# The state-space scan of a hybrid decoder layer: which operand of its last product stands still in TensorE

## The chip, the cores and the metric

The kernel runs on 1 core of one Trainium2 chip. The metric is the device time of one execution in microseconds (us). Every time and row below is of the kernel before the change.

## What is computed

One layer of 256 tokens and 1024 channels: a half-weighted SwiGLU block, a mixer, a second half-weighted SwiGLU block and a final norm. The mixer projects the normalised input once and feeds 8 attention heads and 16 state-space heads of 64 channels; their outputs are gated, normalised and projected back. The change lies in the state-space heads:

```
a     = dt * A                      # per token and head; dt the step, A negative
decay = exp(segsum(a))              # decay[l, s] = exp(cs[l] - cs[s]) for s <= l, 0 above
CB    = einsum('bclgn,bcsgn->bgcls', C, B)
y     = einsum('bgrcls,bcsgrp->bclgrp', CB * decay, x * dt)
y     = y + x * D_skip
y     = y * silu(z)                 # then normalised by group of 8 heads
```

Here cs is the running sum of a over the tokens. With one chunk of 256 tokens the carried states add nothing. All of it is float32.

## The kernel before, in words

Every engine runs one written-out list of work, and semaphores join the lists. The order within a list is the order of execution. The time is mostly weight products on TensorE. Each weight is split into a high and a low part in a type of reduced precision (fp32r), and each product is three matmuls (helper `three`, L1606 to L1608). ACT writes the high part (L634), VectorE the low part (L1085).

The mixer's weights come in 44 half chunks, m = 0 to 43, 1024 columns each. All engines step through m. In the part of interest, m = 20 to 31, one half chunk is 12 matmuls of 512 columns on TensorE (`chunk_half`), and the splits run four steps ahead. Between the half chunks the rest of the mixer is put in: the scan, the transposes of q and k behind m = 22 and 26, the transposes of the gated output behind 27, the attention scores from 28 on.

The scan works on two heads behind each half chunk, m = 20 to 27. For head h there are three 128 by 128 tiles of a triangular matrix: tokens s on partitions, tokens l along columns, the first tile row with both l tiles (256 columns), the second with one (128 columns), 384 columns in all.

- ACT, `decay_exp`: two Relus (L935) make the arguments, one exponential (L939) the decay. Buffers `decay[:, h % 2, :]`. The row cs (`cs_row`) was stored and read back by POOL's queue, spread over all partitions. In step m this stands behind the high split.
- VectorE, `weigh`: two operations (L1472) multiply C B, the step of token s, and the decay, into `mix_m[:, h % 2, :]`. In step m this stands behind the low split, but ahead of it in m = 24.
- TensorE, `ssd_out`: three f32 matmuls a head (L1892 to L1894). A tile of `mix_m`, 128 columns, stands still and 64 columns of `x_tok` move. The outputs, tokens on partitions, fill banks 6 and 7, eight heads a block.
- VectorE, `ssd_add`: in m = 24 and 28 it adds a block of eight heads to x times D_skip (L1481), which POOL wrote (L603). `ssd_gate` (L1489) multiplies by silu(z), and `mix_scale` (L1497) is the norm's last step; the transposes behind m = 27 wait for it.

POOL's queue holds, in this order: the mask of C B, the store and the spreading of cs, four products with D_skip, the rotation of q, the rotation of k.

An f32 matmul leaves two LDWEIGHTS and two MATMUL records in the trace, here called parts; an fp32r matmul and an f32 transpose leave one of each.

Of the kernel before, what the change touches and what calls it, by code (L numbers as in the profile page):

```python
# [17 lines left out]
P = 128  # L18
# [77 lines left out]
def build(nc, x_in, w1s, w3s, w2s, norms, w_in, conv_w, conv_b, dt_bias, A_log, D_skip,  # L96
# [4 lines left out]
    with ExitStack() as ctx:  # L101
# [56 lines left out]
        with ExitStack() as mixer:  # L158
            xbc, qT, kT = (mixer.enter_context(nc.sbuf_tensor(name, shape, f32)) for name, shape in (
                ("xbc", [P, CT, SEQ]), ("qT", [P, HEADS // 2, SEQ]), ("kT", [P, HEADS // 2, SEQ])))  # L160
        sums_hi = sb("sums_hi", [P, 3, 512], f32r)
# [16 lines left out]
        G_BANK, U_BANK = 4, 5  # L178
        PAIR_T_BANK = 6
# [103 lines left out]
        x_tok_ready = sem("x_tok_ready")  # L283
        skip_ready = sem("skip_ready")
        proj_out = sem("proj_out")
        decay_arg = sem("decay_arg")
        decay_ready = sem("decay_ready")
        m_ready = sem("m_ready")
        y_done = sem("y_done")
        y_added = sem("y_added")  # L290
# [169 lines left out]
        def _(pool):  # L460
# [139 lines left out]
            for t in range(TT):  # L600
                for j in range(2):
                    pool.wait_ge(x_tok_ready, 2 * j + t + 1)
                    pool.tensor_tensor(  # L603
                        normed[:, t, D_ATTN + j * 512:D_ATTN + (j + 1) * 512].rearrange("p (h d) -> p h d", d=SP_),
                        x_tok[:, t, j * 512:(j + 1) * 512].rearrange("p (h d) -> p h d", d=SP_),
                        skip16[:, 8 * j:8 * j + 8].unsqueeze(2).to_broadcast([P, 8, SP_]), ALU.mult).then_inc(skip_ready, 1)
            pool.wait_ge(consts_loaded, 16)
            pool.wait_ge(proj_out, 4)
            rotate(q_tok)
            pool.wait_ge(proj_out, 6)  # L610
# [18 lines left out]
        def _(act):  # L629
# [297 lines left out]
            def decay_exp(h0):  # L927

                if h0 % 4 == 0:
                    act.wait_ge(cs_loaded[h0 // 4], 16)  # L930
                for h in (h0, h0 + 1):
                    if h >= 2:
                        act.wait_ge(m_ready, 2 * (h - 1))
                    for s, (a, b) in enumerate(((0, 256), (256, 384))):
                        act.activation(decay[:, h % 2, a:b], cs_row(h)[:, s * P:], ACT.Relu,  # L935
                                       bias=dts[:, 7, s, h:h + 1], scale=-1.0).then_inc(decay_arg, 1)
                for h in (h0, h0 + 1):
                    act.wait_ge(decay_arg, 2 * (h + 1))
                    act.activation(decay[:, h % 2, :], decay[:, h % 2, :], ACT.Exp, scale=-1.0).then_inc(decay_ready, 1)  # L939
# [35 lines left out]
            for m in range(5, MIX_HALVES):  # L975
# [11 lines left out]
                if m in (29, 31, 32):  # L987
                    h = {29: 0, 31: 4, 32: 6}[m]
                    softmax_exp(h)
                    softmax_exp(h + 1)  # L990
                for split in splits(m):
                    mix_hi(split)
# [20 lines left out]
                if 20 <= m < 28:  # L1013
                    decay_exp(2 * (m - 20))
                if m == 20:
                    for t in range(TT):
                        chunk_out("q", t, ACT.Copy, q_tok)
# [52 lines left out]
        def _(dve):  # L1070
# [368 lines left out]
            def cumsum_T_out():  # L1439
                dve.wait_ge(csT_done, 1)  # L1440
                dve.tensor_copy(csT[:, :], bank[0:SH, 7, 0:SEQ]).then_inc(csT_ready, 1)
# [20 lines left out]

            def weigh(h):

                g = h // 8
                if h == 0:
                    dve.wait_ge(cb_masked, 2)
                if h >= 2:
                    dve.wait_ge(y_done, h - 1)
                dve.wait_ge(decay_ready, h + 1)  # L1470
                for s, (a, b) in enumerate(((0, 256), (256, 384))):
                    dve.scalar_tensor_tensor(mix_m[:, h % 2, a:b], cb[:, g, a:b], dts[:, 6, s, h:h + 1],  # L1472
                                             decay[:, h % 2, a:b], ALU.mult, ALU.mult).then_inc(m_ready, 1)

            def ssd_add(g):

                cols = slice(D_ATTN + 512 * g, D_ATTN + 512 * (g + 1))
                dve.wait_ge(y_done, 8 * (g + 1))
                dve.wait_ge(skip_ready, 4)
                for t in range(TT):  # L1480
                    dve.tensor_tensor(normed[:, t, cols], bank[:, 6 + t, :], normed[:, t, cols], ALU.add).then_inc(y_added, 1)  # L1481

            def ssd_gate(g):

                cols = slice(D_ATTN + 512 * g, D_ATTN + 512 * (g + 1))
                for t in range(TT):
                    dve.wait_ge(y_added, 2 * g + t + 1)
                    dve.wait_ge(proj_out, 8 if g else 2)
                    dve.tensor_tensor(normed[:, t, cols], normed[:, t, cols], z_silu[:, t, 512 * g:512 * (g + 1)],  # L1489
                                      ALU.mult).then_inc(gated, 1)  # L1490
# [36 lines left out]
            for m in range(5, MIX_HALVES):  # L1527
                if m in (24, 28):
                    ssd_add(m // 4 - 6)
# [3 lines left out]
                if m == 24:  # L1533
                    weigh(8)
                    weigh(9)
# [15 lines left out]
                if 20 <= m < 28 and m != 24:  # L1551
                    weigh(2 * (m - 20))
                    weigh(2 * (m - 20) + 1)
# [49 lines left out]
        def _(pe):  # L1603
# [281 lines left out]
            def ssd_out(h):  # L1885
                pe.wait_ge(m_ready, 2 * (h + 1))
                if h == 0:
                    pe.wait_ge(x_tok_ready, 4)
                if h == 8:
                    pe.wait_ge(y_added, 2)  # L1890
                m, c, o = mix_m[:, h % 2, :], slice(h * SP_, (h + 1) * SP_), slice((h % 8) * SP_, (h % 8 + 1) * SP_)
                pe.matmul(bank[:, 6, o], m[:, 0:P], x_tok[:, 0, c], start=True, stop=True)  # L1892
                pe.matmul(bank[:, 7, o], m[:, P:SEQ], x_tok[:, 0, c], start=True, stop=False)  # L1893
                pe.matmul(bank[:, 7, o], m[:, SEQ:SEQ + P], x_tok[:, 1, c], start=False, stop=True).then_inc(y_done, 1)  # L1894
# [42 lines left out]
            def pv(h):  # L1937
                pe.wait_ge(probsT_ready, h + 1)
                if h == 0:
                    pe.wait_ge(proj_out, 10)  # L1940
                    pe.wait_ge(y_added, 4)
                pt, c = probsT[:, h, :], slice(h * HD, (h + 1) * HD)
                pe.matmul(bank[:, 6, c], pt[:, 0:P], v_tok[:, 0, c], start=True, stop=True)
                pe.matmul(bank[:, 7, c], pt[:, P:SEQ], v_tok[:, 0, c], start=True, stop=False)
                pe.matmul(bank[:, 7, c], pt[:, SEQ:SEQ + P], v_tok[:, 1, c], start=False, stop=True).then_inc(pv_done, 1)
# [42 lines left out]
            for m in range(M_CONV, M_OUT + 8):  # L1988
# [16 lines left out]
                if m == 18:  # L2005
                    x_transposes(1)
                if 20 <= m < 28:
                    ssd_out(2 * (m - 20))
                    ssd_out(2 * (m - 20) + 1)
# [121 lines left out]
```

## Time and profile before

| what | us |
|---|---|
| median of 3 runs | 550.88 (550.64 to 551.34) |
| profiled execution | 551.28 |
| its span, from first to last instruction | 549.5 |
| TensorE busy | 535.8 |
| VectorE busy | 434.7 |
| ACT busy | 339.4 |

The trace is of one execution. TensorE's matmuls overlap, so the distance from one start to the next says more than a duration. In a row, `128*128 128x512` are the rows and columns that stand still and the shape of what moves; `x4` merges four records, and then the time is from the first start to the last end. PEld is TensorE loading what stands still.

### The profile page before, as it was taken

How to read it: one execution, taken by the hardware profiler on the slowest of the kernel's cores; microseconds unless marked ns; L12 is line 12 of the kernel's file. 1: busy time of each engine (PE TensorE's matmuls, PEld its weight loads, DVE VectorE, ACT ScalarE, POOL GpSimd, SP SyncE). 2: the span in 40 equal slices, each digit the busy share in tenths (PEclk: the TensorE clock that was granted, in tenths of full speed). 3: DMA queues.
4: the chain of work that ended last, by engine and by line, in shares of the span. 5: the costliest groups of instructions: out<-in, count | busy, mean ns of one | idle time of the engine just before them, and what ended most of it. 6: DMA issues, size and time to landing. Idle time of an engine off the chain costs nothing.

```text
span 549.5 us, 9708 instructions
## 1 busy us (share of the span) xinstructions
PE 535.8 (98%) x3637; PEld 491.1 (89%) x3637; DVE 434.7 (79%) x657; ACT 339.4 (62%) x553; POOL 68.6 (12%) x104
## 2 busy tenths in 40 slices
PE   8999999999999989999999999999999999999994
PEld 6999899999999968998888788889999999999993
DVE  4899888889888695778768756599998988888855
ACT  7856466556655565766988864477566556556533
POOL 2003000000000330343741102000000000000015
PEclk9999999999999999999999999999999999999998
DMA  9866955557765327458626244265675557755202
GB/s 269 293 229 217 306 188 196 173 174 227 229 178 183 98 80 228 154 177 287 227 79 229 78 151 155 79 207 166 211 256 188 174 177 229 229 177 182 98 1 76
DMA packets 69966, 99.70 MB, mean 181 GB/s; under 512 B 1941, under 2 KB 55393, under 8 KB 69938
## 3 DMA queue, kind: packets, MB, share of 16 engines
q1 hardware_dynamic: 68336, 94.48, 52.7%
q0 software_dynamic: 1456, 4.59, 2.7%
q8 instruction: 16, 0.26, 0.2%
q10 hardware_dynamic: 146, 0.27, 0.1%
q14 instruction: 12, 0.10, 0.0%
HBM read 98.27 MB, written 1.06 MB: 181 GB/s over the span
## 4 chain that ended last, share of the span: by engine, by line
PE 84%; DVE 6%; DMA 3%; ACT 2%; POOL 2%; issue 2%; SPq 0%; POOLq 0%; DVEq 0%; ACTq 0%
PE bank L1606 26%; PE bank L1607 25%; PE bank L1608 25%; DMA raw<-in_ffn_w 3%; PE bank L1747 1%; DVE w_lo L1085 1%; DVE x L1102 1%; PE bank L1893 1%; PE bank L1894 1%; POOL x L549 1%; PE bank L1892 1%; POOL rstd L482 1%; ACT w_hi L634 1%; PE bank L1933 0%; DVE hT_lo L1148 0%
## 5 line engine op out<-in xcount | busy, mean ns | idle before, releaser
L1606 PE MATMUL bank<-hT_hi,w_hi 128*128 128x256 f32 x736 | 208.7, 284 | 0.8 <-DVE tok_rows L1253 0.7
L1607 PE MATMUL bank<-hT_lo,w_hi 128*128 128x256 f32 x736 | 208.1, 283 | 0.0
L1608 PE MATMUL bank<-hT_hi,w_lo 128*128 128x256 f32 x736 | 208.1, 283 | 0.0
L1085 DVE TENSOR_TENSOR w_lo<-raw,w_hi 128x1024 fp32r<-128x1024 f32 x128 | 158.2, 1239 | 23.4 <-ACT w_hi L634 22.7
L634 ACT ACTIVATE w_hi<-raw 128x1024 fp32r<-128x1024 f32 x128 | 134.0, 1055 | 40.4 <-PE bank L1608 25.6
L1606 PEld LDWEIGHTS bank<-hT_hi,w_hi 128*128 128x128 f32 x736 | 140.9, 191 | 3.5 <-DVE tok_rows L1253 1.7
L1607 PEld LDWEIGHTS bank<-hT_lo,w_hi 128*128 128x128 f32 x736 | 141.0, 192 | 1.5
L1608 PEld LDWEIGHTS bank<-hT_hi,w_lo 128*128 128x128 f32 x736 | 141.0, 192 | 0.0
L1606 PE MATMUL bank<-w_hi,hT_hi 128*128 128x512 f32 (+1 forms) x192 | 70.5, 367 | 1.8 <-DVE hT_lo L1148 0.7
L1608 PE MATMUL bank<-w_hi,hT_lo 128*128 128x512 f32 (+1 forms) x192 | 68.2, 355 | 0.0
L1607 PE MATMUL bank<-w_lo,hT_hi 128*128 128x512 f32 (+1 forms) x192 | 68.0, 354 | 0.0
L751 ACT ACTIVATE conv_acc<-bank 128x256 f32<-128x256 f32 x40 | 15.4, 384 | 63.1 <-PE bank L1608 63.1
L549 POOL TENSOR_TENSOR x<-x_tok,x 128x512 f32<-128x512 f32 x7 | 11.4, 1645 | 303.8 <-ACT x_tok L746 297.3
L1201 DVE TENSOR_TENSOR sums_lo<-x_tok,sums_hi 128x1536 fp32r<-128x1536 f32 x20 | 35.1, 1757 | 12.1 <-ACT sums_hi L716 11.9
L1606 PEld LDWEIGHTS bank<-w_hi,hT_hi 128*128 128x128 f32 x192 | 36.3, 189 | 8.1 <-issue 2.5
L1608 PEld LDWEIGHTS bank<-w_hi,hT_lo 128*128 128x128 f32 x192 | 36.3, 189 | 5.2
L716 ACT ACTIVATE sums_hi<-x_tok 128x1536 fp32r<-128x1536 f32 x20 | 29.7, 1486 | 17.4 <-PE bank L1608 17.4
L1607 PEld LDWEIGHTS bank<-w_lo,hT_hi 128*128 128x128 f32 x192 | 36.4, 190 | 4.3
L1253 DVE TENSOR_TENSOR tok_rows<-bank,conv_acc 128x256 f32<-128x256 f32 x40 | 16.8, 421 | 18.4 <-ACT conv_acc L751 18.4
L1606 PE MATMUL bank<-w_hi,gu_hi 128*128 128x512 f32 x76 | 29.8, 393 | 0.0
L1607 PE MATMUL bank<-w_lo,gu_hi 128*128 128x512 f32 x76 | 29.8, 392 | 0.0
L1608 PE MATMUL bank<-w_hi,gu_lo 128*128 128x512 f32 x76 | 29.6, 389 | 0.0
(223 smaller groups left out, 804.9 us busy)
## 6 DMA issues: line engine op xcount, KB each, us to landing
raw<-in_ffn_w SPq DMA_DIRECT2D x54, 1024.0 KB, 5.4
raw<-in_w_in SPq DMA_DIRECT2D x16, 1024.0 KB, 5.5
tok_rows<-in_ffn_w SPq DMA_DIRECT2D x10, 1024.0 KB, 5.3
raw<-in_w_out SPq DMA_DIRECT2D x6, 1024.0 KB, 4.9
raw<-in_ffn_w SPq DMA_DIRECT2D x8, 256.0 KB, 5.3
x<-in_x SPq DMA_DIRECT2D x4, 256.0 KB, 4.0
norm_w<-cs_heads POOLq DMA_DIRECT2D x2, 512.0 KB, 5.0
out_x<-normed SPq DMA_DIRECT2D x3, 256.0 KB, 2.3
```

What stands on the lines that cost most here:

```text
L482: pool.tensor_tensor(rstd[:, r:r + 1], row_mean[:, r:r + 1], minus_half[:, :], ALU.pow).then_inc(rstd_ready, 1)
L549: pool.tensor_tensor(xs, w2_sum[:, part, :], xs, ALU.add).then_inc(folded, 1)
L634: act.activation(by_tile(dst) if columns else dst, src, ACT.Copy).then_inc(hi_ready, 1)
L716: act.activation(sums_hi[:, :, :], w2_sum[:, 0:3, :], ACT.Copy).then_inc(sums_hi_ready, 1)
L751: act.activation(silu_g, bank[:, GU_BANK, 0:SEQ], ACT.Silu).then_inc(silu_ready, 1)
L1085: dve.tensor_tensor(lo, src, hi, ALU.subtract).then_inc(half_ready, 1)
L1102: dve.scalar_tensor_tensor(xs, bank[:, 2 * t + c, :], 1.0 if n == 2 else 0.5, xs, ALU.mult, ALU.add).then_inc(x_ready, 1)
L1201: dve.tensor_tensor(sums_lo[:, :, :], w2_sum[:, 0:3, :], sums_hi[:, :, :].bitcast(f32), ALU.subtract).then_inc(sums_ready, 1)
L1253: dve.tensor_tensor(gu[:, odd, :], bank[:, GU_BANK, SEQ:], silu_g, ALU.mult).then_inc(gu_ready, 1)
L1606: pe.matmul(dst, lhs[0], rhs[0], start=start, stop=False, skip_group_check=True)
L1607: pe.matmul(dst, lhs[0], rhs[1], start=False, stop=False, skip_group_check=True)
L1608: return pe.matmul(dst, lhs[1], rhs[0], start=False, stop=stop, skip_group_check=True)
```

## The change

- `ssd_out` takes two heads at once. Now x times the step (`xdt`, 64 columns a head) stands still and the tile of the matrix, 128 columns, moves. The output has channels on partitions: head 2p goes to partitions 0 to 63, head 2p + 1 to 64 to 127, both in bank 6, in one of two halves by p.
- VectorE copies that out (`yT_copy`), and TensorE transposes it back to tokens on partitions (`y_transposes`, two 128 by 128 transposes a pair, into bank 7); `y_add` adds it to x times D_skip, once for each pair in place of once for each block.
- The step moves out of `weigh`: `xdt_out` multiplies x by it, in m = 18 and 23, and `weigh` is one product of 384 columns.
- The sign of cs is turned when it is copied, so the Relus need no scale. ACT makes the first 256 columns of the argument, VectorE the last 128 (`decay_last`).
- Order: on ACT `decay_exp` stands ahead of the high split for m = 21 to 27. On VectorE `weigh`, `decay_last`, `yT_copy` and `y_add` stand ahead of the low split. In POOL's queue the second half of the products with D_skip moves behind the rotation of q.

```diff
+        xdt = [xbc[:, first:first + 4, :].rearrange("p (t a) l -> p t (a l)", t=TT) for first in (8, 0)]
+        yT = xbc[:, 4:6, :]
+        YT_BANK, Y_BANK = 6, 7
...
-            for t in range(TT):
-                for j in range(2):
+            def skip(j):
+                for t in range(TT):
                     pool.wait_ge(x_tok_ready, 2 * j + t + 1)
...
+            skip(0)
             pool.wait_ge(consts_loaded, 16)
             pool.wait_ge(proj_out, 4)
             rotate(q_tok)
+            skip(1)
...
                     if h >= 2:
-                        act.wait_ge(m_ready, 2 * (h - 1))
-                    for s, (a, b) in enumerate(((0, 256), (256, 384))):
-                        act.activation(decay[:, h % 2, a:b], cs_row(h)[:, s * P:], ACT.Relu,
-                                       bias=dts[:, 7, s, h:h + 1], scale=-1.0).then_inc(decay_arg, 1)
+                        act.wait_ge(m_ready, h - 1)
+                    act.activation(decay[:, h % 2, 0:SEQ], cs_row(h), ACT.Relu, bias=dts[:, 7, 0, h:h + 1]).then_inc(decay_arg, 1)
                 for h in (h0, h0 + 1):
-                    act.wait_ge(decay_arg, 2 * (h + 1))
+                    act.wait_ge(decay_arg, h + 1)
+                    act.wait_ge(last_arg, h + 1)
                     act.activation(decay[:, h % 2, :], decay[:, h % 2, :], ACT.Exp, scale=-1.0).then_inc(decay_ready, 1)
...
+                if 21 <= m < 28:
+                    decay_exp(2 * (m - 20))
                 for split in splits(m):
                     mix_hi(split)
...
-                if 20 <= m < 28:
-                    decay_exp(2 * (m - 20))
                 if m == 20:
+                    decay_exp(0)
...
+            def xdt_out(j):
+
+                for t in range(TT):
+                    dve.wait_ge(x_tok_ready, TT * j + t + 1)
+                    dve.tensor_tensor(xdt[j][:, t, :].rearrange("p (h d) -> p h d", d=SP_),
+                                      x_tok[:, t, 512 * j:512 * (j + 1)].rearrange("p (h d) -> p h d", d=SP_),
+                                      dts[:, 6, t, 8 * j:8 * j + 8].unsqueeze(2).to_broadcast([P, 8, SP_]),
+                                      ALU.mult).then_inc(xdt_ready, 1)
+
+            def decay_last(h):
+
+                if h % 4 == 0:
+                    dve.wait_ge(cs_loaded[h // 4], 16)
+                if h >= 2:
+                    dve.wait_ge(m_ready, h - 1)
+                dve.tensor_scalar(decay[:, h % 2, SEQ:SEQ + P], cs_row(h)[:, P:SEQ], dts[:, 7, 1, h:h + 1], 0.0,
+                                  ALU.add, ALU.max).then_inc(last_arg, 1)
...
                 if h >= 2:
-                    dve.wait_ge(y_done, h - 1)
+                    dve.wait_ge(y_done, h // 2)
                 dve.wait_ge(decay_ready, h + 1)
-                for s, (a, b) in enumerate(((0, 256), (256, 384))):
-                    dve.scalar_tensor_tensor(mix_m[:, h % 2, a:b], cb[:, g, a:b], dts[:, 6, s, h:h + 1],
-                                             decay[:, h % 2, a:b], ALU.mult, ALU.mult).then_inc(m_ready, 1)
-
-            def ssd_add(g):
...
+                dve.tensor_tensor(mix_m[:, h % 2, :], decay[:, h % 2, :], cb[:, h // 8, :], ALU.mult).then_inc(m_ready, 1)
+
+            def yT_copy(p):
+                dve.wait_ge(y_done, p + 1)
+                if p >= 2:
+                    dve.wait_ge(y_back, p - 1)
+                dve.tensor_copy(yT[:, p % 2, :], bank[:, YT_BANK, p % 2 * SEQ:(p % 2 + 1) * SEQ]).then_inc(yT_ready, 1)
+
+            def y_add(p):
+
+                dve.wait_ge(y_back, p + 1)
+                dve.wait_ge(skip_ready, 2 * (p // 4 + 1))
+                part = normed[:, :, D_ATTN + P * p:D_ATTN + P * (p + 1)]
+                y = bank[:, Y_BANK, p % 2 * SEQ:(p % 2 + 1) * SEQ].rearrange("p (t c) -> p t c", t=TT)
+                dve.tensor_tensor(part, y, part, ALU.add).then_inc(y_added, 1)
...
             for m in range(5, MIX_HALVES):
-                if m in (24, 28):
-                    ssd_add(m // 4 - 6)
+                if 20 <= m < 28:
+                    weigh(2 * (m - 20))
+                    weigh(2 * (m - 20) + 1)
+                if 20 <= m < 27:
+                    decay_last(2 * (m - 19))
+                    decay_last(2 * (m - 19) + 1)
+                if 21 <= m < 29:
+                    yT_copy(m - 21)
+                if 22 <= m < 30:
+                    y_add(m - 22)
...
+            def ssd_out(p):
+
+                pe.wait_ge(m_ready, 2 * (p + 1))
+                if p == 0:
                     pe.wait_ge(x_tok_ready, 4)
-                if h == 8:
-                    pe.wait_ge(y_added, 2)
-                m, c, o = mix_m[:, h % 2, :], slice(h * SP_, (h + 1) * SP_), slice((h % 8) * SP_, (h % 8 + 1) * SP_)
-                pe.matmul(bank[:, 6, o], m[:, 0:P], x_tok[:, 0, c], start=True, stop=True)
-                pe.matmul(bank[:, 7, o], m[:, P:SEQ], x_tok[:, 0, c], start=True, stop=False)
-                pe.matmul(bank[:, 7, o], m[:, SEQ:SEQ + P], x_tok[:, 1, c], start=False, stop=True).then_inc(y_done, 1)
+                if p % 4 == 0:
+                    pe.wait_ge(xdt_ready, p // 2 + 2)
+                if p >= 1:
+                    pe.wait_ge(yT_ready, p)
+                heads = [(mix_m[:, h, :], slice((2 * p + h) % 8 * SP_, ((2 * p + h) % 8 + 1) * SP_), slice(h * SP_, (h + 1) * SP_))
+                         for h in range(2)]
+                xs, a = xdt[p // 4], p % 2 * SEQ
+                for t, own, start in ((0, 0, True), (1, 0, True), (1, 1, False)):
+
+                    for m, c, r in heads:
+                        last = pe.matmul(bank[r, YT_BANK, a + t * P:a + (t + 1) * P], xs[:, own, c],
+                                         m[:, (t + own) * P:(t + own + 1) * P], start=start, stop=t == own)
+                last.then_inc(y_done, 1)
+
+            def y_transposes(p):
+                pe.wait_ge(yT_ready, p + 1)
+                if p >= 1:
+                    pe.wait_ge(y_added, p)
+                for t in range(TT):
+                    a = p % 2 * SEQ + t * P
+                    last = pe.transpose(bank[:, Y_BANK, a:a + P], yT[:, p % 2, tok(t)], ident)
+                last.then_inc(y_back, 1)
...
+                if 21 <= m < 29:
+                    y_transposes(m - 21)
                 if 20 <= m < 28:
-                    ssd_out(2 * (m - 20))
-                    ssd_out(2 * (m - 20) + 1)
+                    ssd_out(m - 20)
```

On VectorE the changed steps also put `xdt_out(0)` into m = 18, `decay_last(0)` and `decay_last(1)` into m = 19, and `xdt_out(1)` into m = 23, each behind the split. On TensorE `y_transposes` and `ssd_out` stand behind the half chunk.

## Rows read from the trace of the kernel before

**Rows 1.** the page's totals by engine: busy us, share of the span, instructions

```profile
PE 535.8 (98%) x3637; PEld 491.1 (89%) x3637; DVE 434.7 (79%) x657; ACT 339.4 (62%) x553; POOL 68.6 (12%) x104
```

**Rows 2.** stretches: us, busy us of each engine (instructions), granted clock, DMA share, GB/s

```profile
268.41:299.71 31.30, 31.30 (x194) 27.66 (x194) 23.10 (x42) 26.23 (x59) 12.05 (x20) 1.00 0.49 169
```

**Rows 3.** timeline of TensorE around the first pair of heads: start us, us, what

```profile
266.92 0.40 PE L1608 MATMUL bank<-w_hi,hT_lo 128*128 128x512 f32 x1
267.16 0.33 PE L1892 MATMUL bank<-x_tok,mix_m 128*128 128x64 f32 x2
...
268.41 0.48 PE L1606 MATMUL bank<-w_hi,hT_hi 128*128 128x512 f32 x1
268.73 0.39 PE L1607 MATMUL bank<-w_lo,hT_hi 128*128 128x512 f32 x1
...
271.02 0.40 PE L1608 MATMUL bank<-w_hi,hT_lo 128*128 128x512 f32 x1
```

**Rows 4.** timeline of TensorE, in the first block of attention scores

```profile
303.38 0.39 PE L1923 MATMUL bank<-kT,qT 64*128 64x128 f32 x4
303.60 0.60 PE L1925 MATMUL bank<-kT,qT 64*128 64x256 f32 x4
```

**Rows 5.** timeline of TensorE, a block of scores that stands alone

```profile
308.79 0.39 PE L1608 MATMUL bank<-w_hi,hT_lo 128*128 128x512 f32 x1
309.11 0.49 PE L1923 MATMUL bank<-kT,qT 64*128 64x128 f32 x4
309.43 0.60 PE L1925 MATMUL bank<-kT,qT 64*128 64x256 f32 x4
309.96 0.50 PE L1606 MATMUL bank<-w_hi,hT_hi 128*128 128x512 f32 x1
310.30 0.39 PE L1607 MATMUL bank<-w_lo,hT_hi 128*128 128x512 f32 x1
```

**Rows 6.** three lines by themselves: duration ns min/median/max, first and last start us

```profile
L1785 PEld LDWEIGHTS bank<-hT_hi,wdt_parts x8: 121/121/121, 212.1 to 213.9; 128*48 128x48 f32 x8
...
L1893 PEld LDWEIGHTS bank<-x_tok,mix_m x32: 192/192/192, 267.3 to 298.5; 128*128 128x128 f32 x32
...
L1923 PE MATMUL bank<-kT,qT x16: 269/272/373, 302.6 to 313.8; 64*128 64x128 f32 x16
```

**Rows 7.** timeline of TensorE, eight transposes of q

```profile
294.00 1.05 PE L1908 MATMUL bank<-cst,tok_rows 128*128 128x128 f32 x8
294.81 0.48 PE L1606 MATMUL bank<-w_hi,hT_hi 128*128 128x512 f32 x1
```

**Rows 8.** VectorE's groups by shape: busy us, mean ns | idle before

```profile
L1085 DVE TENSOR_TENSOR w_lo<-raw,w_hi 128x1024 fp32r<-128x1024 f32 x128 | 158.2, 1239 | 23.4 <-ACT w_hi L634 22.7
...
L1253 DVE TENSOR_TENSOR tok_rows<-bank,conv_acc 128x256 f32<-128x256 f32 x40 | 16.8, 421 | 18.4 <-ACT conv_acc L751 18.4
...
L1472 DVE SCALAR_TENSOR_TENSOR mix_m<-cb,dts,decay 128x256 f32<-128x256 f32 x16 | 8.8, 552 | 2.6 <-ACT decay L939 2.5
...
L1472 DVE SCALAR_TENSOR_TENSOR mix_m<-cb,dts,decay 128x128 f32<-128x128 f32 x16 | 6.1, 380 | 0.0
...
L1497 DVE SCALAR_TENSOR_TENSOR normed<-normed,rstd,mix_w 128x512 f32<-128x512 f32 x6 | 4.3, 747 | 0.4 <-POOL rstd L505 0.4
...
L1489 DVE TENSOR_TENSOR normed<-normed,z_silu 128x512 f32<-128x512 f32 x4 | 2.6, 680 | 0.0
...
L1135 DVE TENSOR_SCALAR normed<-normed,rstd 128x512 f32<-128x512 f32 x3 | 1.5, 486 | 1.7 <-POOL rstd L482 1.7
```

**Rows 9.** timeline of POOL and VectorE, 256 to 300 us

```profile
262.33 4.03 POOL L603 TENSOR_TENSOR normed<-x_tok,small 128x512 f32<-128x512 f32 x3 [3.27 <-ACT x_tok L925]
...
263.72 1.74 DVE L1085 TENSOR_TENSOR w_lo<-raw,w_hi 128x1024 fp32r<-128x1024 f32 x1 [2.21 <-ACT w_hi L634]
...
289.03 1.28 DVE L1489 TENSOR_TENSOR normed<-normed,z_silu 128x512 f32<-128x512 f32 x2
```

**Rows 10.** ACT's groups by shape, 255 to 300 us

```profile
L935 ACT ACTIVATE decay<-norm_w,dts 128x128 f32<-128x128 f32 x8 | 3.1, 394 | 0.0
```

More of the change, by code:

```diff
@@ L283, in build @@
         x_tok_ready = sem("x_tok_ready")
+        xdt_ready = sem("xdt_ready")
         skip_ready = sem("skip_ready")
@@ L286, in build @@
         decay_arg = sem("decay_arg")
+        last_arg = sem("last_arg")
         decay_ready = sem("decay_ready")
@@ L289, in build @@
         y_done = sem("y_done")
+        yT_ready = sem("yT_ready")
+        y_back = sem("y_back")
         y_added = sem("y_added")
@@ L1440, in cumsum_T_out @@
                 dve.wait_ge(csT_done, 1)
-                dve.tensor_copy(csT[:, :], bank[0:SH, 7, 0:SEQ]).then_inc(csT_ready, 1)
+                dve.tensor_scalar(csT[:, :], bank[0:SH, 7, 0:SEQ], -1.0, None, ALU.mult).then_inc(csT_ready, 1)
             def conv_taps(j0):
@@ L1461, in conv_taps @@
                             ins.then_inc(taps_done, 1)
+            def xdt_out(j):
[12 more added lines that the diff above has]
+                                  ALU.add, ALU.max).then_inc(last_arg, 1)
             def weigh(h):
-                g = h // 8
                 if h == 0:
@@ L1468, in weigh @@
                 if h >= 2:
-                    dve.wait_ge(y_done, h - 1)
+                    dve.wait_ge(y_done, h // 2)
                 dve.wait_ge(decay_ready, h + 1)
-                for s, (a, b) in enumerate(((0, 256), (256, 384))):
-                    dve.scalar_tensor_tensor(mix_m[:, h % 2, a:b], cb[:, g, a:b], dts[:, 6, s, h:h + 1],
-                                             decay[:, h % 2, a:b], ALU.mult, ALU.mult).then_inc(m_ready, 1)
-            def ssd_add(g):
[L1477 to L1481, printed above, removed]
+                dve.tensor_tensor(mix_m[:, h % 2, :], decay[:, h % 2, :], cb[:, h // 8, :], ALU.mult).then_inc(m_ready, 1)
[10 more added lines that the diff above has]
+                dve.tensor_tensor(part, y, part, ALU.add).then_inc(y_added, 1)
             def ssd_gate(g):
@@ L1486, in ssd_gate @@
                 for t in range(TT):
-                    dve.wait_ge(y_added, 2 * g + t + 1)
+                    dve.wait_ge(y_added, 4 * (g + 1))
                     dve.wait_ge(proj_out, 8 if g else 2)
@@ L1532, in _ @@
                         hT_lo_part(8 + t + 1, 4 + t, 8, t)
-                if m == 24:
-                    weigh(8)
-                    weigh(9)
                 if m == 29:
@@ L1550, in _ @@
                     cumsum_T_out()
-                if 20 <= m < 28 and m != 24:
-                    weigh(2 * (m - 20))
-                    weigh(2 * (m - 20) + 1)
+                if m == 18:
+                    xdt_out(0)
+                if m == 19:
+                    decay_last(0)
+                    decay_last(1)
+                if m == 23:
+                    xdt_out(1)
                 if m == 25:
@@ L1883, in chunk_half @@
                 chunk_part(m, 1).then_inc(half_used, 1)
-            def ssd_out(h):
-                pe.wait_ge(m_ready, 2 * (h + 1))
-                if h == 0:
+            def ssd_out(p):
+                pe.wait_ge(m_ready, 2 * (p + 1))
+                if p == 0:
                     pe.wait_ge(x_tok_ready, 4)
-                if h == 8:
-                    pe.wait_ge(y_added, 2)
-                m, c, o = mix_m[:, h % 2, :], slice(h * SP_, (h + 1) * SP_), slice((h % 8) * SP_, (h % 8 + 1) * SP_)
-                pe.matmul(bank[:, 6, o], m[:, 0:P], x_tok[:, 0, c], start=True, stop=True)
-                pe.matmul(bank[:, 7, o], m[:, P:SEQ], x_tok[:, 0, c], start=True, stop=False)
-                pe.matmul(bank[:, 7, o], m[:, SEQ:SEQ + P], x_tok[:, 1, c], start=False, stop=True).then_inc(y_done, 1)
+                if p % 4 == 0:
[18 more added lines that the diff above has]
+                last.then_inc(y_back, 1)
             def mix_transposes(count, col, free, free_count):
@@ L1940, in pv @@
                     pe.wait_ge(proj_out, 10)
-                    pe.wait_ge(y_added, 4)
+                    pe.wait_ge(y_added, 8)
                 pt, c = probsT[:, h, :], slice(h * HD, (h + 1) * HD)
```

## The prediction

> **What bounds the kernel now.** I read the page's totals first: TensorE is busy 98% of a span of 549.5 us [rows 1]. So a gain has to be a gain in TensorE's own stream, and any other engine only matters where it makes TensorE wait. Then the table by stretches, for the 31.3 us from the end of the first pair of scan heads to the end of the last: TensorE busy for all of it at a granted clock of 1.00 (the upper of its two levels, 2.4 GHz), ACT busy for 26.23, VectorE for 23.10 [rows 2]. VectorE and ACT both have room there, but not much more than 8 and 5 us. The changed heads lie in this stretch and just ahead of it, a pair of them behind each half chunk of the projection.
>
> Then the timeline of TensorE around one pair [rows 3]. The reader is to see the spacing of the starts, not the durations, for matmuls overlap. One f32 matmul leaves two parts in the trace (L1892 has x2 for one head). The pair starts at 267.16 and the chunk comes back at 268.41: 1.25 us for 6 matmuls, 12 parts, 0.104 us each. Behind the pair the chunk's first matmul takes 0.32 until the next start, where 0.23 is usual. From the last matmul ahead (266.92) to the second behind (268.73) it is 1.81, less two usual steps of 0.23 (ten of them lie between 268.73 and 271.02): **1.35 us for a pair, 10.8 us for the eight.** This is the sum that the change rewrites.
>
> **What a pair costs after it.** Three terms.
>
> (a) The matmuls. Each head keeps its 3 matmuls, but 64 columns stand still (x times the step) and 128 move; the two heads of a pair write partitions 0 to 63 and 64 to 127 of one bank, so each uses half of TensorE's columns. No row of before shows two half-width matmuls by columns. The nearest one splits by rows: the attention scores, 64 rows and 128 columns, two heads beside each other. There 4 parts with 128 moving columns (2 heads) take 0.22 us, from 303.38 to 303.60 [rows 4], which is 0.11 for a part of each head at once. If the columns split as the rows do, a pair is 6 such steps: 0.66 us. If they don't, it is 12: 1.32 us. I take 0.66, as the row is near: the same type, the same number of moving columns, the same half array.
>
> (b) Going into the split array and back. A scores block that stands alone shows it [rows 5]: last chunk matmul at 308.79, second one behind at 310.30, 1.51 in all, less 0.46 for two usual steps is 1.05. Its content by rows 4 is 0.22 + 0.43 = 0.65, since the 256-column matmuls take twice as long as the 128-column ones. So **0.40 us of each visit is the two switches**: TensorE starts the first weights only when the array is empty, and the first matmul on each side has its weights still to load. Eight visits, 3.2 us, are new. The loads may be shorter here: 48 columns loaded in 121 ns, 128 in 192 [rows 6], so 64 should take about 0.13, some 0.06 less. The bounds of a visit are 0 (no switch is needed) and 0.40; I take 0.37, the scores' price with half of the shorter load.
>
> (c) Two new transposes a pair. Eight take 0.80 (294.00 to 294.81) [rows 7], so two take 0.20; they run on the whole array, like the chunk ahead of them, and open no further switch.
>
> Sum: 0.66 + 0.37 + 0.20 = 1.23 against 1.35, so 0.12 less a pair, 1.0 for eight. The scores' price unreduced would give 1.26 and 0.7 less.
>
> The Trainium skill, TensorEngine Tiling (Array Packing), Performance Considerations, recommends just this edit where the moving side has 64 columns or fewer: swap the sides and split the columns, for up to twice the speed; its Key Properties add that a change of tiling mode drains the engine. The last agrees with the 0.40 of [rows 5]. By the first rule alone a pair would take half of 1.35, and the kernel would gain 5.4 us; with the switch and the transposes most of that is gone.
>
> **VectorE.** Per pair it loses 4 scalar_tensor_tensor (two of 256 columns at 0.55, two of 128 at 0.38) and gets 2 products of 384 columns, 2 tensor_scalar of 128, the copy of yT out of PSUM and the addition, 256 columns each. By [rows 8], between 0.42 for 256 columns and 0.68 for 512, a product of 384 takes 0.55; a tensor_scalar of 128 some 0.25 (0.49 for 512); copy and addition 0.42 each. In full durations: 1.10 + 0.50 + 0.84 = 2.44, and 3.68 with the weight split of 1.24. Operations that follow one another overlap by 0.08 (two of 0.68 take 1.28 [rows 9]), so for seven of them 3.1 is nearer. TensorE's round will be 2.84 for the chunk (268.41 to 271.02, and a step) and 1.2 for the rest: 4.0. VectorE fits. Once each come the x times step products (2 x 0.68, half of them ahead of the stretch), the gate (2 x 0.68) and the scale (2 x 0.75); against them fall the two block additions of 2 x 0.68 each. For 8 rounds that is 8 x 3.1 + 1.4 + 1.4 + 1.5 = 29 against 33.5 of TensorE with the q and k transposes.
>
> What TensorE waits for is not the whole round but its first part. Both weigh calls of pair p need pair p-1 finished (as before, but now up to its last matmul); behind them in VectorE's queue stand decay_last twice, yT_copy and y_add, and only then can the transposes of pair p-1 start, which stand ahead of ssd_out(p) and so of the next chunk. That chain is 2.0 to 2.44 us and starts as the chunk of 2.84 starts. It is covered with 0.4 to 0.8 to spare. In the rounds behind xdt_out(1), behind the gate, and while POOL rotates k, some of that goes. POOL does slow VectorE: with POOL's multiplications running from 262.33 to 266.4, the split at 263.72 took 1.74 where 1.24 is the mean [rows 9]. I charge 0.2 for such waits in the eight rounds, and for the mix transposes behind pair 7, which need mix_scale: there VectorE has 0.8 us more in front of it. Bounds 0 and 0.8. What comes off: little stalls in pairs 4 and 5, about 0.1.
>
> **ACT and POOL.** ACT loses two Relus of 128 columns a pair (0.39 each, 6.2 us in all) [rows 10] and keeps the one of 256 and the exponential of each head. It was not waited for, so this gives nothing. The exponentials now also need decay_last, which runs in VectorE's round before, right behind the weigh calls; ACT's first Relu of a pair waits for the same ones. Moving decay_exp ahead of the weight split delays that split by 1.8 us or less; it is used four chunks later, some 16 us. The SP queue loads by those splits, with the same slack. In POOL's queue skip(1) moves behind rotate(q): rotate(q) waited for q from ACT anyway, and skip(1) is wanted at pair 4, some 15 us later. POOL's multiplications go away from the time in which the first products of the scan were slow. In front of the first pair, xdt_out(0) puts 1.3 us on VectorE around 260, where it had idled 2.2 us by 263.72 [rows 9]. All of this I cost at nothing. Behind the scan, y_add(7) is done 20 us ahead of the first PV matmul that takes its bank.
>
> **Result.** The profiled execution took 551.28 with a span of 549.5, so 1.8 lie around the span and are not touched; the median of the runs is 550.88. In the profiled one: 551.28 - 1.0 - 0.1 + 0.2 = 550.4. From the median: **550.0 us**.
>
> **Rivals.**
> (1) The switches cost little by columns. For it: no row shows a column switch. Against it: the row switch does cost 0.40. At half price 8 x 0.19 comes off, 548.5; at none 547.0.
> (2) The change doesn't do what it says: the heads' matmuls run one after the other. For it: no row shows them together. Then (a) is 1.32, 0.66 more for each of eight pairs, 5.3 in all: 555.3, slower. It decides as soon as more than a sixth of the overlap is missing.
> (3) They run together, but each part's weight load is no longer hidden behind the matmul ahead of it. The first part in a split array, where the load is open, takes 373 ns against 272 [rows 5, 6]: 0.10 more. Six steps a pair at 0.05 (a half-width load) to 0.10, eight pairs: 2.4 to 4.8, 552.4 to 554.8. Against it: in the scores the second part of each head shows no such gap. The Trainium skill, TensorE: Matmul & The Clock Gate, Part 3, The mechanism, says that weight loads overlap running matmuls only where the row group differs, and two column tiles share their rows; by that rule this rival would hold, though the same page lets a load go ahead into the background buffer, as the ordinary stream here shows.
> (4) VectorE's chain ends last, ahead of y_transposes. It decides when the chain passes 2.84 us; at 3.1 in every round it costs 8 x 0.3, 552.4; in three rounds 550.9.
>
> **How the numbers follow.** My forecast 0.52, with its own range 549.2 to 550.9; (1) 0.13; (2) 0.12; (3) 0.10; (4) 0.13. A measurement of this kernel can tell about 0.2%, 1.1 us, from no change: the border is 549.8. Of the forecast a bit under half lies below it. Faster 0.23 + 0.13 = 0.36; slower (2), (3) and two thirds of (4), 0.31; same 0.33. The range runs from 548.0 (past the half price of (1)) to 554.9 (past (3), into (2)), and leaves out some 0.15.
>
> **What would show it.** In the changed profile: the two heads' matmuls of a pair starting within hundredths of a us of each other, and a step of 0.11 between such couples (0.22 means (2), 0.16 to 0.21 means (3)); about 0.3 us between the last transpose and the second step, and 0.34 behind the first chunk matmul (0.23 means (1)); rounds of 4.0 us where 4.1 stood; no wait of TensorE on y_add or yT_copy above 0.2. I'd be wrong first in (a) and (b), which both rest on a split by rows, and next in how much VectorE's chain stretches beside POOL.

## The result and the profile after

The changed kernel takes 551.87 us (median of 12 runs, 551.07 to 553.85); the kernel before took 551.15 in 12 runs beside it. The ratio is 1.0019 with a 95% interval of 1.001 to 1.0028: slower, by about 1.0 us, where 1 us faster was forecast. The profiled execution took 551.84, its span is 549.7. The difference is within 0.2%, but on the wrong side of zero, and the interval leaves 1 out.

To see where the time went, I measure one stretch in each profile: from the last chunk matmul ahead of the first pair of heads to the first attention score. Everything that the change puts on TensorE lies in it, the last transposes too, and what the span does elsewhere (the stretch starts some tenths earlier or later from run to run) is left out. Before, it goes from 266.92 [rows 3] to the first score at 302.62, 35.70 us:

```profile
302.62 0.49 PE L1923 MATMUL bank<-kT,qT 64*128 64x128 f32 x4
```

The timeline of TensorE after, with the first pair, one pair in quiet, that is with no wait around it (the transposes of the pair ahead of it, L1953, stand in front), and the first score (L1983):

```profile
266.41 0.39 PE L1651 MATMUL bank<-w_hi,hT_lo 128*128 128x512 f32 x1
266.73 0.88 PE L1943 MATMUL bank<-mix_m,xbc 128*64 128x128 f32 x12
...
284.15 0.39 PE L1651 MATMUL bank<-w_hi,hT_lo 128*128 128x512 f32 x1
284.38 0.38 PE L1953 MATMUL bank<-cst,xbc 128*128 128x128 f32 x2
284.69 0.88 PE L1943 MATMUL bank<-mix_m,xbc 128*64 128x128 f32 x12
285.49 0.50 PE L1649 MATMUL bank<-w_hi,hT_hi 128*128 128x512 f32 x1
285.83 0.40 PE L1650 MATMUL bank<-w_lo,hT_hi 128*128 128x512 f32 x1
...
302.60 0.49 PE L1983 MATMUL bank<-kT,qT 64*128 64x128 f32 x4
```

The stretch is now 36.19 us, 0.49 longer. The pair in quiet is what was forecast: from 284.15 to 285.83 it is 1.68, less two steps of 0.23 is 1.22, where [rows 3] gave 1.35. The 12 parts take 0.88 from the first start to the last end; one of them alone lasts 0.27, so the last starts 0.6 behind the first. One behind the other they would need some 1.2. So the two heads run side by side, in steps of about 0.11.

So the matmuls gave what they should, and something else took more. The stretch from chunk to chunk that answers to [rows 2], with the busy times of TensorE, its loads, VectorE, ACT and POOL:

```profile
267.53:299.45 31.92, 30.83 (x209) 23.93 (x207) 29.51 (x54) 22.77 (x43) 15.33 (x22) 1.00 0.42 148
```

TensorE was busy for all of its 31.30 before; now it idles 1.09 of 31.92. VectorE went from 23.10 to 29.51. The place of the idle time, ahead of the transposes of pair 1 (behind m = 22), in the timeline of all engines:

```profile
271.52 0.50 PE L1649 MATMUL bank<-w_hi,hT_hi 128*128 128x512 f32 x1
271.56 2.35 POOL L612 TENSOR_TENSOR normed<-x_tok,small 128x512 f32<-128x512 f32 x2
...
271.64 2.69 DVE L1501 TENSOR_TENSOR mix_m<-decay,cb 128x384 f32<-128x384 f32 x2 [0.36 <-PE bank L1943]
...
274.25 0.47 DVE L1491 TENSOR_SCALAR decay<-norm_w,dts 128x128 f32<-128x128 f32 x2
...
274.65 0.41 DVE L1507 COPY xbc<-bank 128x256 f32<-128x256 f32 x1
...
274.98 0.41 DVE L1515 TENSOR_TENSOR normed<-bank,normed 128x256 f32<-128x256 f32 x1
...
275.54 0.41 PE L1953 MATMUL bank<-cst,xbc 128*128 128x128 f32 x2 [0.96 <-DVE normed L1515]
...
276.80 1.03 DVE L1501 TENSOR_TENSOR mix_m<-decay,cb 128x384 f32<-128x384 f32 x2 [0.28 <-PE bank L1943]
```

Read it from below. The same two products of `weigh` take 1.03 in the next round and 2.69 in this one, and during just that time POOL runs skip(1) (L612), the D_skip products that the change moved behind the rotation of q. They should have ended 1.66 sooner. The chain behind them (decay_last, the copy of pair 1, the addition of pair 0) ends that much late, and TensorE, done with its chunk, waits 0.96 for the addition. From the first matmul of that chunk (271.52) to the transposes (275.54) it is 4.02; with POOL's products elsewhere it is 2.86 (first experiment), so the delay costs 1.16. A second, smaller wait stands in front of the transposes of pair 5, behind ssd_gate: the same distance is 3.15 there, where 2.90 is usual.

The pairs are counted here as the kernel does: behind half chunk m, TensorE transposes pair m - 21 and multiplies pair m - 20. The expectations below give other names to the same places: where they say the transposes of pair 0, it is those of pair 1, which wait for the addition of pair 0; the products of pair 1 are those of pair 2; and "in front of pair 6" is ahead of the transposes of pair 5.

The stretch is not all of it. The time of a run less the span of its trace is 1.80 us in the median for the kernel before, and 2.07 for the changed one. So of the 0.72 us between the two medians 0.49 is the stretch, by the profiles, and 0.27 lies around the span.

### The profile page after: what moved, and what is told of

It is laid out like the page before. It is cut to its first block, busy times and chain, and to the rows that moved or that the text cites. A ratio compares the mean times of both kernels' runs of the same rounds, so it can differ in the third digit from the quotient of the medians.

```text
span 549.7 us, 9784 instructions
## 1 busy us (share of the span) xinstructions
PE 535.0 (97%) x3653; PEld 486.4 (88%) x3653; DVE 441.2 (80%) x673; ACT 335.9 (61%) x537; POOL 69.1 (13%) x104
## 3 DMA queue, kind: packets, MB, share of 16 engines
HBM read 98.27 MB, written 1.06 MB: 181 GB/s over the span
## 4 chain that ended last, share of the span: by engine, by line
PE 85%; DVE 6%; DMA 3%; issue 2%; ACT 2%; POOL 1%; POOLq 0%; DVEq 0%; SPq 0%; ACTq 0%
PE bank L1649 26%; PE bank L1650 26%; PE bank L1651 26%; DMA raw<-in_ffn_w 3%; DVE w_lo L1098 1%; PE bank L1790 1%; PE bank L1943 1%; DVE x L1115 1%; PE bank L1813 1%; POOL rstd L491 1%; ACT w_hi L646 1%; PE bank L1993 0%; DVE hT_lo L1161 0%; PE bank L1953 0%; PE bank L1968 0%
```

## The experiments

All numbers called "stretch" are the time defined above, from one profile of each kernel: 35.70 before, 36.19 changed. Kernels whose list on TensorE is the same and where no wait differs give it within 0.03 (35.70 and 35.73, 35.08 and 35.07, 34.36 twice). A "round" is from the last matmul of one chunk to the last of the next.

**Where POOL's products stand.** Three places, and nearly none of them.

```diff
             skip(0)
+            skip(1)
             pool.wait_ge(consts_loaded, 16)
             pool.wait_ge(proj_out, 4)
             rotate(q_tok)
-            skip(1)
```

> The changed kernel with the second half of the D_skip products back in front of the rotation of q in POOL's queue. Theory (POOL's products beside VectorE's first product of pair 1 hold VectorE up, and TensorE waits 0.96 us in front of the transposes of pair 0): the wait of 0.96 us is gone, the kernel is 1.0 us faster than the changed one, 550.1 to 550.8 where before is 551.15. Rival (the wait has another cause, VectorE's chain is too long anyway): the wait stays above 0.5 us and the time stays near 551.9. A side effect to look for: the first products of the scan, which then meet POOL's products, may end after the chunk of m = 20, up to 0.5 us lost.

550.75 us, ratio 0.9991 (0.9979 to 1.0002) to before; stretch 35.08, 1.11 less than changed. The timeline of VectorE, with two decay_last ahead of the scan and the same two products of `weigh`, and what is left of TensorE's waits for VectorE's copy or addition at the transposes:

```profile
262.35 2.06 DVE L1491 TENSOR_SCALAR decay<-norm_w,dts 128x128 f32<-128x128 f32 x2
...
271.14 1.29 DVE L1501 TENSOR_TENSOR mix_m<-decay,cb 128x384 f32<-128x384 f32 x2 [0.22 <-PE bank L1943]
```

```profile
PEld bank L1953 <- DVE xbc L1507: 0.8, 2, 0.5
```

The theory holds. The wait of 0.96 is gone, and the side effect cost nothing: POOL's products now run ahead of the scan, and what they hold up there is two decay_last (2.06 us in place of 0.47). The products of pair 0 still end ahead of the chunk of m = 20.

The second kernel cuts skip(1) to one channel a head and leaves the order as changed. So heads 8 to 15 lack most of x times D_skip.

```diff
+            pool.memset(normed[:, :, D_ATTN + 512:], 0.0)
...
-                        normed[:, t, ...].rearrange("p (h d) -> p h d", d=SP_),
+                        normed[:, t, ...].rearrange("p (h d) -> p h d", d=SP_)[:, :, 0:SP_ if j == 0 else 1],
...
```

> The changed kernel with the second half of the D_skip products cut to one of 64 channels per head (the rest of heads 8 to 15 gets no x times D_skip; the place is filled with zeros at the start). Order of the queues as in the changed kernel. Theory (contention with POOL's two long products): as without any conflict, the wait of 0.96 us goes to under 0.1, time 550.3 to 550.9. It bounds what any other place for these products can give. Rival (order or chain length): the wait stays above 0.5 us.

551.32 us, ratio 1.0005 (0.999 to 1.0021). That is above the expected 550.3 to 550.9, and the interval is too wide to tell it from before or from the changed kernel; but the stretch is 35.07, the same as with the products in front, and the wait of 0.96 is gone. So what hurt is the two long products, not the order of POOL's queue, and in front they cost nothing.

The third puts the products behind the rotation of k.

```diff
             rotate(q_tok)
-            skip(1)
             pool.wait_ge(proj_out, 6)
             rotate(k_tok)
+            skip(1)
```

> The changed kernel with the second half of the D_skip products behind the rotation of k, at about 287 to 290 us, and the transposes where the change put them. Theory (what hurts is POOL's long products beside VectorE's chain, wherever they stand): the wait of 0.96 us in front of the transposes of pair 0 is gone, and one of 0.7 us or more appears in front of the transposes of pair 4 or 5, on top of the 0.4 us of the wait that is there already; time within 0.5 us of the changed kernel, 551.4 to 552.2. Rival (only the place behind the rotation of q is bad): the wait moves nowhere, 550.5 to 550.9.

552.09 us, ratio 1.0017 (1.0007 to 1.0028); stretch 36.06. The timeline of the third place:

```profile
285.91 1.49 DVE L1491 TENSOR_SCALAR decay<-z_silu,dts 128x128 f32<-128x128 f32 x2
...
286.28 2.04 POOL L612 TENSOR_TENSOR normed<-x_tok,small 128x512 f32<-128x512 f32 x2
...
287.32 0.41 DVE L1507 COPY xbc<-bank 128x256 f32<-128x256 f32 x1
287.65 0.41 DVE L1515 TENSOR_TENSOR normed<-bank,normed 128x256 f32<-128x256 f32 x1
...
288.21 0.41 PE L1953 MATMUL bank<-cst,xbc 128*128 128x128 f32 x2 [0.58 <-DVE normed L1515]
```

Now it is the two decay_last that take 1.49 instead of 0.47, and TensorE waits in front of pair 4's transposes. The wait moved with the products, as the theory says. The profile puts it at 0.58 and not 0.7, while the distance from the chunk's first matmul to the transposes grew by 0.74 (3.64 in place of 2.90); the next round, still late, waits 0.37.

**The same move without the new chain.** The kernel before, with skip(1) behind rotate(q) as in the change:

```diff
-            for t in range(TT):
-                for j in range(2):
+            def skip(j):
+                for t in range(TT):
...
+            skip(0)
             pool.wait_ge(consts_loaded, 16)
             pool.wait_ge(proj_out, 4)
             rotate(q_tok)
+            skip(1)
```

> The kernel before with only the move in POOL's queue: second half of the D_skip products behind the rotation of q. Theory (the move only hurts together with the new chain on VectorE): POOL's products meet VectorE at 272 to 275 us there too, but before the change the products of a pair have the whole chunk as cover, so TensorE waits less than 0.3 us; time within 0.3 us of before. Rival (the move alone costs 1 us): 552.1.

551.05 us, ratio 0.9998 (0.9983 to 1.0013); stretch 35.73. POOL's two products and what VectorE does beside them:

```profile
271.25 3.07 POOL L603 TENSOR_TENSOR normed<-x_tok,small 128x512 f32<-128x512 f32 x2
```

```profile
271.36 2.06 DVE L1087 TENSOR_TENSOR w_lo<-raw,w_hi 128x1024 fp32r<-128x1024 f32 x1
273.34 2.18 DVE L1474 SCALAR_TENSOR_TENSOR mix_m<-cb,dts,decay 128x256 f32<-128x256 f32 x4
```

The products slow VectorE here too: a weight split takes 2.06 in place of 1.21, four operations of `weigh` 2.18 in place of 1.41. TensorE doesn't notice. The move alone is free; the move with a chain that fills most of the chunk costs 1 us.

**The order on TensorE.**

```diff
+                if 20 <= m < 28:
+                    ssd_out(m - 20)
                 if 21 <= m < 29:
                     y_transposes(m - 21)
-                if 20 <= m < 28:
-                    ssd_out(m - 20)
```

> The changed kernel with the transposes of pair p - 1 behind ssd_out(p) and not ahead of it. ssd_out still waits for the copy of pair p - 1. Theory (VectorE's chain of two products, two decay_last, copy, addition ends too late for what stands first behind the chunk): the additions now have 0.8 us more, the copy ends 0.33 us earlier than the addition; the wait of 0.96 us falls to about 0.6, that of 0.33 us in front of pair 6 to under 0.1, 0.5 to 0.7 us faster than the changed kernel, 551.2. Rival (order costs nothing because the addition is not what TensorE waits for): no difference beyond 0.2 us.

550.91 us, ratio 0.9995 (0.998 to 1.001); stretch 34.98, 1.21 less than changed, where 0.5 to 0.7 was expected. The waits fell as expected, to 0.52 and nothing. The rest is the round: 3.92 in place of 4.01 in quiet, which I had not foreseen. By the times the gain is 1.0 us. With the products in front as well:

> Both together: the D_skip products in front and the transposes of pair p - 1 behind ssd_out(p). Theory: the wait in front of pair 6 (0.4 us) goes, and each round falls from 4.01 to 3.92 as in the run with the swap alone; together 1.0 us less than with the products in front alone, 549.6 to 550.0. Rival (the swap only moves waits about): 550.5 to 550.9.

549.79 us, ratio 0.9987 (0.9978 to 0.9996); stretch 34.36, another 0.7 less than with the products in front alone, where 1.0 was expected. The kernel before took 550.78 beside it. Its timeline, one round:

```profile
279.91 0.47 PE L1649 MATMUL bank<-w_hi,hT_hi 128*128 128x512 f32 x1
...
282.51 0.39 PE L1651 MATMUL bank<-w_hi,hT_lo 128*128 128x512 f32 x1
282.83 0.88 PE L1943 MATMUL bank<-mix_m,xbc 128*64 128x128 f32 x12
283.64 0.44 PE L1953 MATMUL bank<-cst,xbc 128*128 128x128 f32 x2
283.83 0.47 PE L1649 MATMUL bank<-w_hi,hT_hi 128*128 128x512 f32 x1
284.15 0.39 PE L1650 MATMUL bank<-w_lo,hT_hi 128*128 128x512 f32 x1
```

From 282.51 to 284.15, less 0.46, is 1.18 for a pair with its transposes (1.22 in the other order), and no wait for VectorE is left. Then yT_copy ahead of decay_last on top:

```diff
+                if 21 <= m < 29:
+                    yT_copy(m - 21)
                 if 20 <= m < 27:
                     decay_last(2 * (m - 19))
                     decay_last(2 * (m - 19) + 1)
-                if 21 <= m < 29:
-                    yT_copy(m - 21)
```

> As the one before, and on VectorE yT_copy stands ahead of the two decay_last. Theory: what TensorE can wait for in front of ssd_out ends 0.4 us earlier, but in the run before there is nothing left to wait for, so no difference beyond 0.2 us. If it is 0.3 us or more faster, VectorE's chain was still at the edge.

549.86 us, ratio 0.9981 (0.9972 to 0.999); stretch 34.36, to the hundredth the same. There was nothing left to wait for.

**What the split array costs.** Both on the kernel with the products in front (stretch 35.08), one run each. First the two heads in turn:

```diff
-                for t, own, start in ((0, 0, True), (1, 0, True), (1, 1, False)):
-                    for m, c, r in heads:
+                for m, c, r in heads:
+                    for t, own, start in ((0, 0, True), (1, 0, True), (1, 1, False)):
```

> On the kernel with the D_skip products in front: in ssd_out the three matmuls of one head, then the three of the other, not alternating. Theory (TensorE starts matmuls in the order of the queue, and two overlap only if they follow one another and use different columns): only the last of the first head and the first of the second overlap, 10 steps of 0.11 in place of 6, 0.44 us more a pair, 3.5 us in all, 554.3; the 12 parts take 1.3 us and not 0.88 in the timeline. Rival (either half of the array runs by itself, whatever the order in the queue): no change.

552.4 us in the one run, and not 554.3; stretch 36.84, 1.76 more. The order in the queue does decide how much the halves overlap, but less sharply than I said: 0.27 a pair, not 0.44.

```profile
284.87 1.14 PE L1942 MATMUL bank<-mix_m,xbc 128*64 128x128 f32 x12
```

1.14 in place of 0.88, so about 8 steps and not 10. The records don't name the head, but from 0.27 behind the first start on they begin in twos: there the second head came in, while two of the first head's three matmuls were still to come or running.

The other kernel goes into the split array once more for each pair:

```diff
                 for t, own, start in ((0, 0, True), (1, 0, True), (1, 1, False)):
+                    if (t, own) == (1, 0) and p >= 1:
+                        y_transposes(p - 1)
                     for m, c, r in heads:
...
-                if 21 <= m < 29:
+                if m == 28:
                     y_transposes(m - 21)
```

> On the kernel with the D_skip products in front: the two transposes of pair p - 1 stand in the middle of ssd_out(p), behind the first two of its six matmuls, for p = 1 to 7. No work is added, only seven more changes from half columns to the whole array and back. Theory (a visit to the split array costs 0.37 us by its two switches): 7 x 0.3 to 0.37 more, 2.1 to 2.6 us, 552.9 to 553.4. Rival (columns need no switch, and what stands around the matmuls comes from somewhere else): under 0.7 us more.

552.0 us in the one run, stretch 36.80: 1.72 more than with the products in front, less than the 2.1 to 2.6 expected, and well over the rival's 0.7. With the transposes in the middle the wait of 0.25 in front of pair 5's is gone too, so seven visits cost 1.97, 0.28 each. Against the kernel that has the transposes behind ssd_out, where TensorE waits for VectorE as little as here, it is 2.44 more, 0.35 each. The two differ by what the order itself is worth, under 0.1 a round. The timeline shows one visit:

```profile
283.79 0.44 PE L1944 MATMUL bank<-mix_m,xbc 128*64 128x128 f32 x4
284.16 0.44 PE L1954 MATMUL bank<-cst,xbc 128*128 128x128 f32 x2
284.53 0.66 PE L1944 MATMUL bank<-mix_m,xbc 128*64 128x128 f32 x8
```

Four parts side by side are 0.22 of work and stand 0.37 in front of the transposes; these are 0.20 and stand 0.37 in front of the rest. That is 0.15 and 0.17 for the two switches, 0.32 together, between the two figures above.

**ACT's order.** On the kernel with both (the products in front, the transposes behind ssd_out), decay_exp behind the high split again:

```diff
-                if 21 <= m < 28:
-                    decay_exp(2 * (m - 20))
                 for split in splits(m):
                     mix_hi(split)
...
+                if 20 <= m < 28:
+                    decay_exp(2 * (m - 20))
                 if m == 20:
-                    decay_exp(0)
```

> On the kernel with the D_skip products in front and the transposes behind ssd_out: ACT's decay_exp back behind the high split for m = 21 to 27, as before the change. Theory (ACT is ahead of what TensorE and VectorE want from it, so its order is worth nothing): no difference beyond 0.2 us to the run with front and swap, rounds of 3.92 us. Rival (decay_exp was put ahead because VectorE's products would wait for it): VectorE's products wait for the exponentials 0.5 us or more in several rounds, and where the chain passes the chunk TensorE waits too: 0.5 to 2 us more.

550.46 us, ratio 0.999 (0.9979 to 1.0001), not told apart by the times from the run that it was made from; the stretch tells them apart: 35.09, 0.73 more. One round is 4.64 in place of 3.92, the one with the products of pair 1, which wait for the copy of pair 0. Its timeline:

```profile
268.72 1.06 ACT L646 ACTIVATE w_hi<-raw 128x1024 fp32r<-128x1024 f32 x1
...
269.67 0.90 ACT L947 ACTIVATE decay<-norm_w,dts 128x256 f32<-128x256 f32 x2
...
270.47 0.93 ACT L951 ACTIVATE decay<-decay 128x384 f32<-128x384 f32 x2
271.09 1.45 DVE L1500 TENSOR_TENSOR mix_m<-decay,cb 128x384 f32<-128x384 f32 x2 [1.11 <-ACT decay L951]
...
273.48 0.88 PE L1942 MATMUL bank<-mix_m,xbc 128*64 128x128 f32 x12 [0.64 <-DVE xbc L1506]
```

The rival is right for one round. ACT writes out q first in that round, then the split of 1.06 comes, and the exponentials of pair 1 stand behind it; later ACT is ahead again and the order is worth nothing.

## Why the prediction was wrong

- **TensorE's sum, (a), (b), (c): right.** Forecast 1.23 a pair, measured 1.22. Halves by columns overlap as halves by rows did, steps of 0.11 as in [rows 4]. A visit was taken at 0.37; adding seven gave 0.28 or 0.35 each, by which kernel one compares with. Over the stretch: 36.19, less 1.16 and 0.25 for the two waits, is 34.78, so 0.9 came off against a forecast of 1.0, and 0.1 for small stalls. The side with no switch cost (rival 1) and the two with lost overlap are out: (2) needed steps of 0.22, (3) of 0.16 to 0.21, so the loads of the half arrays are hidden.
- **The step that failed is the cost of POOL's queue: "POOL's multiplications go away from the time in which the first products of the scan were slow [...] All of this I cost at nothing."** I said where they went away from, and not where they went to. They went to 271.6 to 273.9, onto the first operations of a chain that I had myself found to have 0.4 to 0.8 us to spare, while [rows 9] showed that POOL can stretch an operation of VectorE by 0.5. The runs show 1.66 of delay in VectorE, a wait of 0.96, and 1.16 more for the round. With the products in front the step would have been right: 550.75, 1.1 less; and the same stretch comes out when the two long products are only cut short where they stand.
- **VectorE's chain: the mechanism was rival (4), and the sum for its whole round held** (29 us of work forecast, 29.51 busy, with at least 1.7 of contention in it). Its charge of 0.2 in waits was mis-sized: 1.16 and 0.25 in two rounds, 1.4 together, and the bound of 0.8 was too low too. It decided not in every round, as (4) priced it, but in one that POOL entered, and a little in the one behind the gate.
- **ACT: "Moving decay_exp ahead of the weight split [...] All of this I cost at nothing" holds for what the move delays, but the move is needed.** Without it the scan loses 0.73 in its first round, at least in the kernel where nothing else waits there.
- **"1.8 lie around the span and are not touched" did not hold.** It is 1.80 to 1.82 in the median for the kernel before and for the one with only POOL's move, and 2.01 to 2.10 in each of the eight kernels with the new chain that have 10 to 12 runs. What in the change adds these 0.2 to 0.3 us is open.
- The whole sum: forecast was -1.0 - 0.1 + 0.2, 0.9 us faster. Measured were -0.92 + 1.41 in the stretch and 0.27 around the span, 0.76 us slower, where the medians differ by 0.72.
- The range, 548.0 to 554.9, holds 551.87, and the chance for slower was 0.31. The wrong sign comes from one omitted mechanism of 1 us on a net gain of 1 us. With it gone the ratio is 0.9991, and its interval still holds 1: even then the gain is about half of the forecast.

The best of these kernels, the products in front and the transposes behind ssd_out, has 549.79, and 549.86 with the copy first. That is 0.13% and 0.19% under the kernel before, with intervals that leave 1 out, and by the stretch 1.8 us under the changed one.

## What to carry to other kernels

When work is moved in a queue, look up what runs at the place where it arrives, on the engines that it disturbs as well as on its own; a long POOL product beside VectorE can cost VectorE most of its length (here 1.66 of 2.35 us), and whether that is free depends on how much of the cover the chain there already uses. Swapping the still and the moving side to use half columns brought the matmuls of a pair from 1.25 to about 0.66 us, but each visit pays two switches, and here each result had to be turned back; count those first. Put what has slack (here the transposes) behind what has none, and alternate the halves in the queue.

## What the runs showed of the hardware that I had not expected

- VectorE beside two POOL products of 128x512: two products of 384 columns took 2.69 us against 1.03, and two tensor_scalar of 128 columns 1.49 against 0.47. In the first case VectorE lost 1.66 while POOL's two took 2.35. POOL is held up as well: its two take 3.07 in the kernel before with the move, where a long weight split runs beside them.
- Not every operation is held up: in the kernel with the products behind the rotation of k, the copy and the addition, which both read PSUM (`bank`), take 0.41 each beside POOL's product, the same as without it.
- Two half arrays by columns take queued matmuls of one half somewhat past the other: with three of head 0 ahead in the queue, head 1 came in 0.27 us behind head 0, not 0.44 (one run, read from where the starts begin to come in twos).
- A full-array transpose directly behind the chunk, and the split array behind it, made a round of 4.01 us; the other order 3.92. The pair with its transposes accounts for 0.04 of it (1.22 to 1.18); the chunk's own steps were a little slower in the first order (ten of them 2.33 against 2.29). Why is open.
